# Swapping the loops over token halves and over products in the one-slot matmul helper

## Chip, cores and metric

One NeuronCore of a Trainium2 chip. The metric is the device time of one execution in microseconds; the median of three runs of the kernel before is 2221.11 us (2218.87 to 2223.14).

## The reference

A decoder trunk of two layers runs over 512 prompt tokens and 32 sample tokens (8 sequences of 4) with shared weights, all in float32, model width 1024 and feed-forward width 2816:

```
for i in range(2):
    x += 0.5 * swiglu(rms_norm(x))          # gate, up: 1024 -> 2816, down: 2816 -> 1024
    x += mixer_i(rms_norm(x))               # i = 0: conformer convolution, i = 1: gated linear attention
    x += 0.5 * swiglu(rms_norm(x))
y = rms_norm(x)                             # and the new convolution and attention states
```

The bulk of the arithmetic is the dense products of the four feed-forward blocks and of the mixers' projections.

## The kernel before

**Layout.** Activations stand feature-major in SBUF, 128 features on the partitions and all T = 544 tokens beside each other, so one matmul takes a 128x128 weight block as stationary operand and streams tokens. 544 columns do not fit one PSUM bank of 512 float32 values, so the tokens are cut into two halves of HALF = 272 columns: half c of an output block lies in bank `2 * pair + c`, and a unit of work (one output block of 128 features) owns a pair of banks. The eight banks make four pairs, and units go round them.

**Precision.** Every float32 operand is split into a high part that the matmul's fp32r type holds exactly and a low part with the rest. A product a*w is three matmuls into the same bank: w_hi*a_hi, w_hi*a_lo and w_lo*a_hi.

**Weight slots.** A slot is one block of weights of up to SLOT_K = 8 contraction steps (1024 rows x 128 columns). SyncE loads it with one DMA into `raw` (two buffers, line 386), ScalarE rounds it into `w_hi` (four buffers, line 418), VectorE writes the rest into `w_lo` (line 425) and signals `w_split`. TensorE waits for `w_split`, uses the slot and signals `w_done` on its last matmul. ScalarE waits for `w_done` before it refills a buffer, and VectorE waits for it before it evacuates the pair of banks (lines 649 and 653 in the feed-forward blocks) and signals `evac`, for which TensorE waits before a unit takes a pair again.

**Who uses a slot.** `slot_products` (line 438 is its matmul) handles units that use one slot at a time: per contraction step k six matmuls, now ordered product outside and half inside. Almost all of the kernel goes through it: the gate and up blocks after the first few (`pe_ffn`), all down blocks (three calls of 8, 8 and 6 steps on one pair), the later half of the square projections (`pe_square`) and most projections of the attention mixer. `wide_products` (line 459) handles the first units of a stage, two or four pairs at a time, and has loops of its own. Both helpers issue in program order on TensorE; there is no planner, and the orders on the other engines are written out by hand in their own blocks, tied to TensorE by the semaphores above.

**A place with another order.** In the convolution mixer, `taps` multiplies 512 token columns by diagonal weights (lines 925 and 930), 18 matmuls or more in a row into one bank, each with a weight block of its own, in the same fp32r type.

Of the kernel before, what the change touches and what calls it, by code (L numbers as in the profile page):

```python
# [42 lines left out]
def build(nc, x_prompt, x_sample, state_conv, state_gla, norm_ffn_pre, norm_mix, norm_ffn_post, norm_final,  # L43
# [26 lines left out]
    with ctx:  # L70
# [7 lines left out]
        def sb(name, shape, dt=F32):  # L78
            n = 4
            for d in shape[1:]:  # L80
                n *= d
            offset = taken[0]
            taken[0] += (n + 31) // 32 * 32
            return at(name, shape, dt, offset)
# [10 lines left out]
        w_hi = sb("w_hi", [P, RING, SLOT_K, P], F32R)  # L95
        w_lo = sb("w_lo", [P, RING, SLOT_K, P], F32R)
# [332 lines left out]
        def slot_products(pe, n, pair, a_hi, a_lo, nk=SLOT_K, k0=0, kt=SLOT_K, i=0, per=0, ready=None):  # L429

            pe.wait_ge(w_split, n + 1 + per * i)
            r = n % RING
            for k in range(nk):
                if ready is not None:
                    pe.wait_ge(ready[0], ready[1] + k + 1)
                for w, a in ((w_hi, a_hi), (w_hi, a_lo), (w_lo, a_hi)):
                    for c in range(2):
                        last = nc.tensor.matmul(  # L438
                            ps[:, 2 * pair + c, 0:HALF], w[:, r, k, :], a[:, k0 + k, c * HALF:(c + 1) * HALF],
                            start=(k0 + k == 0 and w is w_hi and a is a_hi),  # L440
                            stop=(k0 + k == kt - 1 and w is w_lo))
            last.then_inc(w_done, 1)
# [31 lines left out]
        def pe_ffn(pe, s):  # L474
            u0, s0 = s.up.u0, s.up.s0
            if s is f00:
                pe.wait_ge(evac, 2)
                pe.wait_ge(s_xo, 2)
                wide_products(pe, s0, [u0 % 4, (u0 + 1) % 4], xg_hi, xg_lo, (x_split, 0))

                pe.wait_ge(s_diag, TT + 1)
                bank = 2 * ((u0 + 3) % 4)
                for t in range(TT):
                    nc.tensor.matmul(ps[:, bank, t * P:(t + 1) * P], ones[:, :], rdiag[:, t, :], start=True, stop=True)
                nc.tensor.matmul(ps[:, bank + 1, 0:NS], ones[:, :], rdiag[:, TT, 0:NS], start=True, stop=True).then_inc(
                    s_stat, 1)
                slot_products(pe, s0 + 2, (u0 + 2) % 4, xg_hi, xg_lo)
                pe.wait_ge(s_r0, 1)
                slot_products(pe, s0 + 3, (u0 + 3) % 4, xg_hi, xg_lo)
            else:  # L490
                pe.wait_ge(evac, u0 - 2)
                wide_products(pe, s0, [u0 % 4, (u0 + 1) % 4], xg_hi, xg_lo, (x_split, M * s.q))
                pe.wait_ge(evac, u0)
                pe_stat(pe, s.e, (u0 + 3) % 4)
                slot_products(pe, s0 + 2, (u0 + 2) % 4, xg_hi, xg_lo)
                pe.wait_ge(s_nv, 3 * s.r + 1)
                slot_products(pe, s0 + 3, (u0 + 3) % 4, xg_hi, xg_lo)
# [1286 lines left out]
```

## Time and profile before

| | |
|---|---|
| median of 3 runs | 2221.11 us |
| profiled execution, its own time | 2221.3 us |
| its span (first to last instruction) | 2219.6 us |
| mean granted TensorE clock | 0.981 of full speed |
| TensorE busy | 2132.1 us, 16225 matmuls |
| TensorE weight loads busy | 2080.0 us, 16225 loads |
| VectorE, ScalarE, GpSimd busy | 1027.1, 732.8, 273.3 us |

Matmuls are pipelined: the duration in a row (some 290 ns) spans filling and draining the array and overlaps the next matmul, so what a matmul costs in a stream is the distance from one start to the next, not its duration. In the timeline, neighbouring instructions of one group are merged into a row with a count; a row "x2" is one product over its two halves.

### The profile page before, as it was taken

The page shows a single profiled execution, that of the slowest core. Times are in us where ns is not written, and L with a number is a line of the kernel's source. Part 1 is how long each engine was busy: PE and PEld are TensorE (multiplying, and loading weights), DVE is VectorE, ACT ScalarE, POOL GpSimd, SP SyncE. Part 2 cuts the span into 40 slices and gives each one's busy share as a digit, 9 for nine tenths or more (in the row PEclk, how much of TensorE's full clock was granted, in tenths as well). Part 3 has the DMA queues.
Part 4 walks back from the last instruction along what each step waited for, and adds up shares of the span by engine and source line. Part 5 has one row for each costly group of instructions (what it writes and reads, how often), then busy time and mean ns, then how long its engine had stood idle before and what let it go on. Part 6 is the DMA issues. An engine that isn't in the chain of part 4 may idle for free.

```text
span 2219.6 us, 39410 instructions
## 1 busy us (share of the span) xinstructions
PE 2132.1 (96%) x16225; PEld 2080.0 (94%) x16225; DVE 1027.1 (46%) x1266; ACT 732.8 (33%) x1132; POOL 273.3 (12%) x222
## 2 busy tenths in 40 slices
PE   8999999888789999999999999999999899999997
PEld 8999999878679999999999999999987799999997
DVE  4444433289966444433254443233455464444322
ACT  5222222376754222222232222222333242222222
POOL 0000001168823000001100000121000030000000
PEclk9999999988899999999999999999999999999999
DMA  4332233311103323322233223332224133332321
GB/s 139 91 89 85 83 88 88 97 39 57 39 24 95 95 85 88 91 82 84 82 98 92 85 85 87 88 91 77 67 58 142 58 96 95 90 90 85 95 79 67
DMA packets 338765, 185.67 MB, mean 84 GB/s; under 512 B 6012, under 2 KB 334942, under 8 KB 338668
## 3 DMA queue, kind: packets, MB, share of 16 engines
q1 hardware_dynamic: 335228, 172.78, 26.9%
q0 software_dynamic: 3200, 11.64, 1.6%
q8 instruction: 60, 0.98, 0.2%
q14 instruction: 21, 0.17, 0.0%
q10 hardware_dynamic: 256, 0.10, 0.0%
HBM read 177.29 MB, written 8.05 MB: 84 GB/s over the span
## 4 chain that ended last, share of the span: by engine, by line
PE 84%; DVE 10%; issue 3%; ACT 2%; DMA 1%; POOL 0%; ACTq 0%; SPq 0%; DVEq 0%
PE ps L438 76%; PE ps L459 4%; DVE ps L1464 3%; DVE w_lo L425 1%; DVE prod L1505 1%; ACT w_hi L418 1%; PE ps L1115 1%; DMA hist_in<-in_state_conv 0%; PE ps L1121 0%; DVE cv L1511 0%; PE ps L1054 0%; DMA pin<-in_gla_onorm_g 0%; PE ps L1062 0%; DVE x L1542 0%; DVE cv L1513 0%
## 5 line engine op out<-in xcount | busy, mean ns | idle before, releaser
L438 PE MATMUL ps<-xg_hi,w_hi 128*128 128x272 f32 x3344 | 696.9, 290 | 4.2 <-DVE tb L1479 2.2
L438 PE MATMUL ps<-xg_hi,w_lo 128*128 128x272 f32 x3344 | 693.6, 289 | 0.0
L438 PE MATMUL ps<-xg_lo,w_hi 128*128 128x272 f32 x3344 | 691.1, 288 | 0.0
L418 ACT ACTIVATE w_hi<-raw 128x1024 fp32r<-128x1024 f32 x329 | 347.7, 1059 | 1020.7 <-PE ps L438 970.3
L425 DVE TENSOR_TENSOR w_lo<-raw,w_hi 128x1024 fp32r<-128x1024 f32 x329 | 425.8, 1296 | 446.3 <-ACT w_hi L418 445.8
L438 PEld LDWEIGHTS ps<-xg_hi,w_hi 128*128 128x128 f32 x3344 | 528.6, 189 | 7.6 <-DVE tb L1479 2.6
L438 PEld LDWEIGHTS ps<-xg_lo,w_hi 128*128 128x128 f32 x3344 | 527.2, 189 | 0.0
L438 PEld LDWEIGHTS ps<-xg_hi,w_lo 128*128 128x128 f32 x3344 | 523.6, 189 | 0.0
L438 PE MATMUL ps<-h_hi,w_hi 128*128 128x272 f32 x1536 | 318.2, 288 | 1.7 <-DVE x L1542 0.9
L438 PE MATMUL ps<-h_hi,w_lo 128*128 128x272 f32 x1536 | 317.9, 288 | 0.0
L438 PE MATMUL ps<-h_lo,w_hi 128*128 128x272 f32 x1536 | 316.7, 288 | 0.0
L438 PEld LDWEIGHTS ps<-h_hi,w_hi 128*128 128x128 f32 x1536 | 241.5, 188 | 2.2 <-DVE x L1542 1.1
L438 PEld LDWEIGHTS ps<-h_lo,w_hi 128*128 128x128 f32 x1536 | 241.4, 188 | 0.0
L438 PEld LDWEIGHTS ps<-h_hi,w_lo 128*128 128x128 f32 x1536 | 239.8, 189 | 0.0
L653 DVE TENSOR_TENSOR tb<-ps,rB 128x544 f32<-128x544 f32 x88 | 63.8, 725 | 298.3 <-PE ps L438 298.3
L805 POOL TENSOR_TENSOR pool_sum<-pool_sum,tap_prod 128x512 f32<-128x512 f32 x89 | 136.0, 1528 | 56.8 <-ACT tap_prod L1260 44.5
L546 POOL TENSOR_TENSOR acc<-x 128x544 f32<-128x544 f32 x5 | 5.5, 1094 | 915.8 <-DVE x L670 854.2
L600 ACT ACTIVATE h_hi<-tb 128x544 f32 x88 | 58.0, 659 | 178.5 <-DVE tb L658 178.5
L649 DVE TENSOR_TENSOR ta<-ps,rB 128x544 f32<-128x544 f32 x88 | 63.8, 725 | 107.5 <-PE ps L438 106.6
L660 DVE TENSOR_TENSOR h_lo<-tb,h_hi 128x544 f32 x88 | 63.8, 725 | 83.9 <-ACT h_hi L600 83.9
L550 POOL TENSOR_TENSOR sqt<-x 128x544 f32<-128x544 f32 x35 | 38.3, 1095 | 315.8 <-DVE x L670 288.4
L925 PE MATMUL ps<-u_hi,diag 128*128 128x512 f32 x120 | 45.0, 548 | 29.8 <-ACT u_hi L1252 29.8
(266 smaller groups left out, 1506.0 us busy)
## 6 DMA issues: line engine op xcount, KB each, us to landing
raw<-in_ffn_w_gate SPq DMA_DIRECT2D x88, 512.0 KB, 3.8
raw<-in_ffn_w_up SPq DMA_DIRECT2D x88, 512.0 KB, 3.8
raw<-in_ffn_w_down SPq DMA_DIRECT2D x64, 512.0 KB, 4.0
raw<-in_gla_w_in SPq DMA_DIRECT2D x25, 512.0 KB, 3.8
raw<-in_ffn_w_down SPq DMA_DIRECT2D x32, 384.0 KB, 3.3
raw<-in_conv_w_pw SPq DMA_DIRECT2D x24, 512.0 KB, 4.0
raw<-in_gla_w_out SPq DMA_DIRECT2D x8, 512.0 KB, 4.0
st<-in_state_gla POOLq DMA_DIRECT2D x4, 1024.0 KB, 9.6
```

The source lines that it names most:

```text
L418: nc.scalar.activation(w_hi[:, n % RING], raw[:, n % RAW], ACT.Copy).then_inc(w_high, 1)
L425: nc.vector.tensor_tensor(w_lo[:, n % RING], raw[:, n % RAW], w_hi[:, n % RING].bitcast(F32), ALU.subtract).then_inc(w_split, 1)
L438: last = nc.tensor.matmul(ps[:, 2 * pair + c, 0:HALF], w[:, r, k, :], a[:, k0 + k, c * HALF:(c + 1) * HALF], start=(k0 + k == 0 and w is w ...
L459: last = nc.tensor.matmul(ps[:, 2 * pair + c, 0:HALF], w[:, r, k, :], a[:, k, c * HALF:(c + 1) * HALF], start=(k == 0 and w is w_hi and a ...
L550: nc.gpsimd.tensor_tensor(sqt[:, :], src[:, m, :], src[:, m, :], ALU.mult).then_inc(p_acc, 1)
L600: nc.scalar.activation(h_hi[:, 2 * i + p, :], tb[:, p, :], ACT.Copy).then_inc(h_high, 1)
L649: nc.vector.tensor_tensor(halves(ta[:, p, :]), bank_pair(pair), halves(rB[:, :]), ALU.mult).then_inc(evac, 1)
L653: nc.vector.tensor_tensor(halves(tb[:, p, :]), bank_pair((pair + 1) % 4), halves(rB[:, :]), ALU.mult).then_inc(evac, 1)
L660: nc.vector.tensor_tensor(h_lo[:, 2 * i + p, :], tb[:, p, :], h_hi[:, 2 * i + p, :].bitcast(F32), ALU.subtract).then_inc(h_split, 1)
L805: nc.gpsimd.tensor_tensor(pool_sum[:, m % 2, :], pool_sum[:, m % 2, :], tap_prod[:, k % PRODS, :], ALU.add).then_inc(c_padd, 1)
L925: last = nc.tensor.matmul(ps[:, 4 + m % 2, :], diag[:, diag_slot(m, j), part, :], u_hi[:, m % 2, j:j + SEQ], start=(j == 0 and part == 0), ...
L1464: last = nc.vector.scalar_tensor_tensor(out=ps[:, bank, :], in0=uext[:, m, j:j + SEQ], scalar=tap(j, m), in1=ps[:, bank, :], op0=ALU.mult, ...
```

## The change

In `slot_products` the loop over the two halves moves outside the loop over the three products. Per contraction step the six matmuls were (product, half) hh0 hh1 hl0 hl1 lh0 lh1, where hh is w_hi*a_hi, hl is w_hi*a_lo, lh is w_lo*a_hi; they become hh0 hl0 lh0 hh1 hl1 lh1. Each bank still receives the same products in the same order, the first matmul still carries `start`, and the last one issued is still lh1, which carries the signal. `wide_products` is left as it is.

```
             for k in range(nk):
                 if ready is not None:
                     pe.wait_ge(ready[0], ready[1] + k + 1)
-                for w, a in ((w_hi, a_hi), (w_hi, a_lo), (w_lo, a_hi)):
-                    for c in range(2):
+                for c in range(2):
+                    for w, a in ((w_hi, a_hi), (w_hi, a_lo), (w_lo, a_hi)):
                         last = nc.tensor.matmul(
                             ps[:, 2 * pair + c, 0:HALF], w[:, r, k, :], a[:, k0 + k, c * HALF:(c + 1) * HALF],
                             start=(k0 + k == 0 and w is w_hi and a is a_hi),
```

## Rows read from the trace of the kernel before

**Rows 1.** The page: span, busy time of each engine, granted clock in 40 slices.

```profile
span 2219.6 us, 39410 instructions
...
PE 2132.1 (96%) x16225; PEld 2080.0 (94%) x16225; DVE 1027.1 (46%) x1266; ACT 732.8 (33%) x1132; POOL 273.3 (12%) x222
...
PEclk9999999988899999999999999999999999999999
```

**Rows 2.** The chain that ended last, by engine and by line.

```profile
PE 84%; DVE 10%; issue 3%; ACT 2%; DMA 1%; POOL 0%; ACTq 0%; SPq 0%; DVEq 0%
...
by line: PE ps L438 76.0%; PE ps L459 3.8%; DVE ps L1464 3.1%; issue 2.5%; DVE w_lo L425 1.5%; DVE prod L1505 1.2%; ACT w_hi L418 1.0%; PE ps L1115 0.6%; DMA hist_in<-in_state_conv 0.5%; PE ps L1121 0.4%; DVE cv L1511 0.4%; PE ps L1054 0.3%
```

**Rows 3.** Instruction groups of line 438: busy us, mean ns, idle before.

```profile
L438 PE MATMUL ps<-xg_hi,w_hi 128*128 128x272 f32 x3344 | 696.9, 290 | 4.2 <-DVE tb L1479 2.2
L438 PE MATMUL ps<-xg_hi,w_lo 128*128 128x272 f32 x3344 | 693.6, 289 | 0.0
L438 PE MATMUL ps<-xg_lo,w_hi 128*128 128x272 f32 x3344 | 691.1, 288 | 0.0
...
L438 PEld LDWEIGHTS ps<-xg_hi,w_hi 128*128 128x128 f32 x3344 | 528.6, 189 | 7.6 <-DVE tb L1479 2.6
...
L438 PE MATMUL ps<-h_hi,w_hi 128*128 128x272 f32 x1536 | 318.2, 288 | 1.7 <-DVE x L1542 0.9
L438 PE MATMUL ps<-h_hi,w_lo 128*128 128x272 f32 x1536 | 317.9, 288 | 0.0
L438 PE MATMUL ps<-h_lo,w_hi 128*128 128x272 f32 x1536 | 316.7, 288 | 0.0
```

**Rows 4.** The chain in order of time, four longest pieces: start us, us, what.

```profile
33.96 384.95 PE ps L438 x3072
...
708.78 384.85 PE ps L438 x3072
...
1106.60 384.86 PE ps L438 x3072
...
1817.20 285.63 PE ps L438 x2280
```

**Rows 5.** Line 438 in a stretch of 100 us: busy, granted clock, DMA share, GB/s.

```profile
1200.00:1300.00 100.00, 100.00 (x801) 100.00 (x800) 1.00 0.30 89
```

**Rows 6.** Timeline of TensorE, eight contraction steps: start us, us, line, group.

```profile
1200.39 0.41 PE L438 MATMUL ps<-xg_hi,w_hi 128*128 128x272 f32 x2
1200.64 0.41 PE L438 MATMUL ps<-xg_lo,w_hi 128*128 128x272 f32 x2
1200.90 0.41 PE L438 MATMUL ps<-xg_hi,w_lo 128*128 128x272 f32 x2
1201.15 0.41 PE L438 MATMUL ps<-xg_hi,w_hi 128*128 128x272 f32 x2
1201.40 0.41 PE L438 MATMUL ps<-xg_lo,w_hi 128*128 128x272 f32 x2
1201.64 0.41 PE L438 MATMUL ps<-xg_hi,w_lo 128*128 128x272 f32 x2
...
1206.41 0.41 PE L438 MATMUL ps<-xg_hi,w_hi 128*128 128x272 f32 x2
```

**Rows 7.** Who waited for whom: us in total, times, longest us.

```profile
ACT w_hi L418 <- PE ps L438: 970.3, 276, 5.9
...
DVE w_lo L425 <- ACT w_hi L418: 445.8, 277, 25.3
DVE tb L653 <- PE ps L438: 298.3, 81, 3.7
```

**Rows 8.** Timeline of TensorE, first channel block of the convolution's taps.

```profile
450.86 2.95 PE L925 MATMUL ps<-u_hi,diag 128*128 128x512 f32 x12
453.64 1.55 PE L930 MATMUL ps<-u_lo,diag 128*128 128x512 f32 x6
455.04 0.42 PE L438 MATMUL ps<-xg_hi,w_hi 128*128 128x272 f32 x2
```

**Rows 9.** The same stretch: TensorE busy, granted clock, DMA share, GB/s.

```profile
450.80:455.10 4.30, 4.30 (x21) 1.00 0.00 0
```

More of the change, by code:

```diff
@@ L435, in slot_products @@
                     pe.wait_ge(ready[0], ready[1] + k + 1)
-                for w, a in ((w_hi, a_hi), (w_hi, a_lo), (w_lo, a_hi)):
-                    for c in range(2):
+                for c in range(2):
+                    for w, a in ((w_hi, a_hi), (w_hi, a_lo), (w_lo, a_hi)):
                         last = nc.tensor.matmul(
```

## The prediction

> **What bounds the kernel now.** I read the page's totals first. TensorE is busy for 2132.1 of 2219.6 us, and there are exactly as many weight loads as matmuls, 16225 of each [rows 1]. A busy row of matmuls overlaps its neighbour, so this says only that TensorE hardly ever stands idle, not how fast it streams. The chain that ended last says where the end comes from: line 438, the line of the change, is 76.0% of it [rows 2], which is 0.760 x 2219.6 = 1687 us. The changed line has 3 x 3344 + 3 x 1536 = 14640 matmuls [rows 3], or 2440 contraction steps of six.
>
> The chain in order of time gives the price of one matmul. Three pieces hold 3072 matmuls in 384.95, 384.85 and 384.86 us, a fourth 2280 in 285.63 us [rows 4]: each comes to 125.3 ns per matmul, with nothing else in the chain between them. So some 1687 / 0.1253 = 13460 of the 14640 stand on the path (2243 steps of six), and the others lie in the convolution and attention stages where other engines end the wait. The granted clock in such a stretch is 1.00, the 2.4 GHz level, with 801 matmuls in 100 us [rows 5]. At one column per cycle 272 columns would take 272 / 2.4 = 113.3 ns; the stream runs 12.0 ns above that. What these 12 ns are is the question of this change, because nothing else in the program is touched. The timeline shows that the step from one product pair to the next is 0.25 us whichever product it is [rows 6].
>
> The other engines have room. ScalarE waits 970.3 us in total for line 438 to release weight buffers, and VectorE 298.3 us for its products to evacuate [rows 7]. They follow TensorE.
>
> **The change, part by part.** Nothing is removed and nothing added: the same 14640 matmuls with the same 14640 weight loads, the same operands, the same six per step. No DMA, no instruction of SP or POOL and no wait moves. The wait for the slot stands before the six, and so does the wait for the activation block where there is one; both already cover all operands of the step, so w_lo being read third instead of fifth can't meet an unfinished split. The signal stays on lh1, which stays last, so refills and evacuations are released where they are now: cost nothing, and no cover is needed for it. Bank c = 0 gets its final product three matmuls (0.38 us) sooner, but nobody is told, so this earns nothing either. Three things differ inside the step.
>
> *One: neighbours in the same bank.* Now every matmul follows one into the other bank. Afterwards hh0-hl0, hl0-lh0, hh1-hl1 and hl1-lh1 are neighbours in one bank, four of six. No row of line 438 shows that order, so I bound it by the nearest row, the convolution's taps: same type, 128x128 weights, 18 matmuls of 512 columns in a row into one bank. They run from 450.86 to 455.04 us [rows 8], 4.18 / 18 = 232.2 ns each, at granted clock 1.00 [rows 9], against 512 / 2.4 = 213.3. That is 18.9 ns above the column time, where the bank-switching stream has 12.0. If the excess is a fixed sum per matmul, the same bank costs at most 18.9 - 12.0 = 6.9 ns. If the excess grows with the columns, the switching stream scaled to 512 would take 125.3 x 512 / 272 = 235.9 ns, the same-bank stream is 3.7 ns better, and scaled back to 272 columns that is 2.0 ns gained. On the path 13460 x 4/6 = 8970 neighbours are concerned: the ends are +62 us and -18 us. I take 0, because the two readings have opposite signs and the true law of the excess (two points, one of 272 and one of 512 columns) most plausibly lies between them: a straight line with an intercept leaves nothing for the bank.
>
> *Two: weight changes.* Now the stationary block differs from the one before twice per step (hl1 to lh0, and lh1 to the next hh0). Afterwards it differs four times, since lh0 stands between two w_hi products. The timeline has both kinds today. A step from the hh row to the hl row holds two starts without a change, the other two kinds of step hold one change each. Over the eight steps from 1200.39 to 1206.41 us [rows 6] the eight hh-to-hl distances sum to 2.02 us, the sixteen others to 4.00 us: 252.5 ns without a change, 250.0 with one. A change costs -2.5 ns, with some 3 ns of uncertainty from rows rounded to 0.01 us, so at most about +0.5. Two more per step on 2243 steps of the path: ends +2 and -12 us (taken at -2.5). I take 0, since the taps of [rows 8] change weights at every matmul and stream no better for it. The reason is plain in the groups: a load is issued for every matmul, changed or not [rows 1, 3].
>
> The Trainium skill has a rule against this change: TensorE: Matmul & The Clock Gate, section Step-by-step, says that loading apart from computing lets one load weights once and matmul repeatedly. By it the old order would need two loads per step and the new one four. The trace doesn't bear it out for this program, which issues six loads in a step; by the rule the sum would be positive, by the row it is 0.
>
> *Three: what streams while what loads.* Now the stream of a_hi runs beside the coming w_hi three times in six, and each other pairing once. Afterwards a_hi beside w_hi four times, a_lo beside w_lo twice. No pairing is new in kind, and all of them lie within the 0.24 to 0.26 us per pair of [rows 6]: 0, inside the bounds of the second point.
>
> The sum is 0 + 0 + 0. The profiled execution took 2221.3 us with a span of 2219.6, 0.2 us from the median of 2221.11 us. I predict 2221.2 us.
>
> **The rivals.** About 0.2%, 4.4 us, is what a measurement of this kernel can tell from no change; divided over 8970 neighbours that is 0.5 ns per matmul. So this is a sharp question, and small effects count.
>
> *Slower by the bank:* a matmul that accumulates into the bank just written pays a fixed fee. For it: the taps' excess of 18.9 against 12.0 ns. Against it: 512 columns are more columns, and their activations are read at shifted offsets, which the dense stream doesn't do. At the full 6.9 ns it is 2221.2 + 62 = 2283 us; it decides from 0.5 ns upwards. Chance 0.06.
>
> *Slower by the weights:* a changed block costs more than a repeated one, but today each change is followed by at least one repeat that absorbs it; with lh0 alone between two changes, it no longer is. For it: a load's row lasts 189 ns [rows 3], longer than the distance of 125.3, so loads must overlap. Against it: the taps change at every matmul, and their excess is at most 6.9 ns more with 512 columns to hide a load in. At 3 ns for each of 2 x 2243 more changes it is 13 us, 2235 us; it decides from 1 ns upwards. Chance 0.06. This is also where the skill's rule of loading once would show.
>
> *Faster by the bank:* the 12.0 ns are the price of going to the other bank after each matmul. Four of six would no longer pay it: 8970 x 12.0 = 108 us, 2114 us. For it: every matmul of line 438 switches, so nothing in that line contradicts it. Against it: the taps never switch in a run of 18 and are further above their column time, not nearer. Chance 0.07, smaller gains such as the 18 us above (2203 us) included.
>
> A change that doesn't do what it says is hard to picture here, as the program is issued in the written order; it would give the forecast's time.
>
> **How the numbers follow.** Forecast, no measurable change: 0.78. The two slower rivals 0.12, the faster one 0.07, and 0.03 for causes that I don't name, two thirds of it slower, where there is more room for mishap. That makes faster 0.08, same 0.78, slower 0.14. The forecast's own band is 2216.8 to 2225.6 us. It holds slightly under 8 in 10, so the range reaches a little into the others: down by 7 us, a gain of 0.8 ns per neighbour in a bank, to 2214; up by 12 us, a fee of 1.3 ns per neighbour or most of the 3 ns per change, to 2233.
>
> **What would show it.** Right: the long pieces of the chain still hold 3072 matmuls in 384.9 us; the line's groups keep their counts; the timeline of a step shows single hh, hl, lh rows twice with starts 0.125 us apart; ScalarE's wait for line 438 stays near 970 us. Bank fee: the distances hh to hl and hl to lh grow while lh0 to hh1 stays at 125. Weight fee: the distances at lh, before and behind, grow while hh to hl stays. Bank gain: hh to hl and hl to lh fall towards 113 ns, and ScalarE's wait shrinks. The prediction is wrong if the pieces of 3072 differ from 384.9 us by more than about 1.0 us (4.4 x 3072 / 13460).

## The result, and the profile after

The changed kernel takes 2232.54 us (2230.46 to 2237.08, five runs) against 2220.93 us (2217.31 to 2223.14) of the kernel before: a ratio of 1.0055, interval 1.0042 to 1.0068. It is slower by 11.6 us, small, but well outside what a measurement can mistake.

The page of the changed kernel, its span and busy times, answers to [rows 1]:

```profile
span 2230.7 us, 39410 instructions
...
PE 2139.9 (96%) x16225; PEld 2087.8 (94%) x16225; DVE 1030.2 (46%) x1266; ACT 732.3 (33%) x1132; POOL 269.8 (12%) x222
```

The counts are the old ones, down to the last instruction: nothing was added, and nothing else was set off. Its chain in order of time, against [rows 4], shows where the time went:

```profile
32.96 387.50 PE ps L438 x3072
...
711.63 387.41 PE ps L438 x3072
...
1112.01 387.43 PE ps L438 x3072
...
1825.81 287.53 PE ps L438 x2280
```

Each piece of 3072 matmuls has 2.55 to 2.57 us more than its partner, the piece of 2280 has 1.90 us more. All four give 0.83 to 0.84 ns per matmul, 126.1 for 125.3, or 5.0 ns per contraction step of six. Over the 13460 matmuls of the path that is 13460 x 0.83 = 11.2 us; the profiled spans differ by 2230.7 - 2219.6 = 11.1 us. The four pieces together, 11496 matmuls, already hold 9.6 us of it. So there is no new wait and no stage to look for: the stream itself is slower, by the same amount in all four pieces that `slot_products` feeds.

The granted clock of such a stretch is still 1.00, the 2.4 GHz level, with 796 matmuls in 100 us for the 801 of [rows 5]:

```profile
1200.00:1300.00 100.00, 100.00 (x796) 100.00 (x794) 1.00 0.31 89
```

The waits of the other engines only stretch with the stream (970.3 us in [rows 7]):

```profile
ACT w_hi L418 <- PE ps L438: 981.4, 276, 5.9
```

And the timeline of a contraction step, against [rows 6], shows the new order as single rows, hh hl lh and again hh hl lh:

```profile
1203.02 0.29 PE L438 MATMUL ps<-xg_hi,w_hi 128*128 128x272 f32 x1
1203.14 0.29 PE L438 MATMUL ps<-xg_lo,w_hi 128*128 128x272 f32 x1
1203.27 0.29 PE L438 MATMUL ps<-xg_hi,w_lo 128*128 128x272 f32 x1
1203.40 0.29 PE L438 MATMUL ps<-xg_hi,w_hi 128*128 128x272 f32 x1
1203.52 0.29 PE L438 MATMUL ps<-xg_lo,w_hi 128*128 128x272 f32 x1
1203.65 0.29 PE L438 MATMUL ps<-xg_hi,w_lo 128*128 128x272 f32 x1
```

A fee of under a nanosecond per matmul can't be read off single starts that are printed to 10 ns. The pieces of 3072 show it: within either of these two runs they agree to 0.1 us. They are the measure in all that follows, old order 384.9 us, new order 387.4 us. Where no interval stands beside a whole time, or only pieces are shown, the kernel was run once.

### The profile page after: what moved, and what is told of

Same layout as the page of the kernel before. It is cut to its first block, busy times and chain, and to the rows that moved or that the text cites. A ratio compares the mean times of both kernels' runs of the same rounds, so it can differ in the third digit from the quotient of the medians.

```text
span 2230.7 us, 39410 instructions
## 1 busy us (share of the span) xinstructions
PE 2139.9 (96%) x16225; PEld 2087.8 (94%) x16225; DVE 1030.2 (46%) x1266; ACT 732.3 (33%) x1132; POOL 269.8 (12%) x222
## 4 chain that ended last, share of the span: by engine, by line
PE 84%; DVE 10%; ACT 2%; issue 2%; DMA 1%; POOL 0%; SPq 0%; ACTq 0%; DVEq 0%
PE ps L438 77%; PE ps L459 4%; DVE ps L1464 3%; DVE w_lo L425 2%; DVE prod L1505 2%; ACT w_hi L418 1%; PE ps L1115 1%; PE ps L1121 0%; DMA hist_in<-in_state_conv 0%; DVE cv L1511 0%; PE ps L1054 0%; DMA pin<-in_gla_onorm_g 0%; PE ps L1062 0%; DVE x L1542 0%; DVE u_lo L1498 0%
## 5 line engine op out<-in xcount | busy, mean ns | idle before, releaser
L438 PE MATMUL ps<-xg_hi,w_hi 128*128 128x272 f32 x3344 | 971.3, 290 | 5.1 <-DVE tb L1479 2.2
L438 PE MATMUL ps<-xg_lo,w_hi 128*128 128x272 f32 x3344 | 967.8, 289 | 0.0
L438 PE MATMUL ps<-xg_hi,w_lo 128*128 128x272 f32 x3344 | 967.5, 289 | 0.0
L438 PEld LDWEIGHTS ps<-xg_hi,w_hi 128*128 128x128 f32 x3344 | 631.5, 189 | 7.9 <-issue 3.2
L438 PEld LDWEIGHTS ps<-xg_lo,w_hi 128*128 128x128 f32 x3344 | 630.6, 189 | 0.8
L438 PEld LDWEIGHTS ps<-xg_hi,w_lo 128*128 128x128 f32 x3344 | 630.8, 189 | 0.0
L438 PE MATMUL ps<-h_hi,w_hi 128*128 128x272 f32 x1536 | 444.4, 289 | 1.7 <-DVE x L1542 0.9
L438 PE MATMUL ps<-h_lo,w_hi 128*128 128x272 f32 x1536 | 443.9, 289 | 0.0
L438 PE MATMUL ps<-h_hi,w_lo 128*128 128x272 f32 x1536 | 443.7, 289 | 0.0
L438 PEld LDWEIGHTS ps<-h_hi,w_lo 128*128 128x128 f32 x1536 | 289.0, 188 | 0.0
## 6 DMA issues: line engine op xcount, KB each, us to landing
raw<-in_ffn_w_down SPq DMA_DIRECT2D x32, 384.0 KB, 3.4
```

What stands on the lines that cost most here:

```text
L438: last = nc.tensor.matmul(ps[:, 2 * pair + c, 0:HALF], w[:, r, k, :], a[:, k0 + k, c * HALF:(c + 1) * HALF], start=(k0 + k == 0 and w is w ...
```

## The experiments

### Bank, weights or streams

Three theories stood at the start. The new order has four neighbours per step in the same bank where the old one has none; it has four changes of the stationary block where the old one has two; and a second half never follows the first half of the same tile any more. Four kernels take these apart. The first, second and fourth edits below are made in the new kernel, the third in the old one; `...` marks lines of an edit that are not shown.

**Banks alternate, the rest as in the new order.**

```
-                for c in range(2):
-                    for w, a in ((w_hi, a_hi), (w_hi, a_lo), (w_lo, a_hi)):
+                hh, hl, lh = (w_hi, a_hi), (w_hi, a_lo), (w_lo, a_hi)
+                order = ((hh, 0), (hl, 1), (lh, 0), (hh, 1), (hl, 0), (lh, 1))
+                for n_mm, ((w, a), c) in enumerate(order):
...
```

> The six matmuls of a step in the order hh0 hl1 lh0 hh1 hl0 lh1: the weight blocks follow each other as in the changed kernel (four changes of block per step), and so does what streams while what loads, but every matmul goes to the other bank than the one before, as in the old kernel. Bank theory (1.25 ns for each same-bank neighbour, none left here): long pieces of the chain 384.9 us for 3072 matmuls, about 2221 us. Weight theory (2.5 ns for each of the two added changes): 387.4 us, about 2232 us. Stream theory (1.7 ns for each lost pair hh0-hh1, hl0-hl1, lh0-lh1 in which the second half follows the first of the same tile): 387.4 us, about 2232 us.

Measured: 2221.41 us, ratio 0.9997 (0.9988 to 1.0007). The chain of this run, in which the matmul stands at line 441:

```profile
710.30 384.85 PE ps L441 x3072
...
1108.12 384.86 PE ps L441 x3072
```

This is the old time exactly, with four weight changes per step and no half that follows its first half. The weight theory and the stream theory as I had put it are gone. Had I stopped here, the bank would have looked guilty.

**Same-bank neighbours with two weight changes.**

```
...
+                order = ((hh, 0), (hl, 0), (hh, 1), (hl, 1), (lh, 1), (lh, 0))
...
```

> Order hh0 hl0 hh1 hl1 lh1 lh0: four same-bank neighbours of six, counting lh0 to the next step's hh0, as in the changed kernel, but only two changes of weight block per step, as in the old one. Bank theory: 387.4 us per 3072 matmuls, about 2232 us. Weight theory: 384.9 us, about 2221 us. Stream theory (no second half follows its first half): 387.4 us, about 2232 us.

Measured: 2223.93 us, ratio 1.0016 (1.0007 to 1.0026). Its chain:

```profile
709.43 385.69 PE ps L441 x3072
...
1108.08 385.71 PE ps L441 x3072
```

It fits none of the three theories: 0.85 us per piece above the old order, a third of the new order's fee, with as many same-bank neighbours.

**One bank for everything, old order of operands.**

```
-                            ps[:, 2 * pair + c, 0:HALF], w[:, r, k, :], a[:, k0 + k, c * HALF:(c + 1) * HALF],
+                            ps[:, 2 * pair, 0:HALF], w[:, r, k, :], a[:, k0 + k, c * HALF:(c + 1) * HALF],
...
```

> The old order of operands throughout, but both halves are summed into the first bank of the pair, so all six matmuls of a step are same-bank neighbours; the second bank keeps old contents (half of the outputs are not the reference's). Bank theory: 6 x 1.25 = 7.5 ns per step, 512 steps in a piece of 3072, so 384.9 + 3.8 = 388.7 us, about 2238 us. Weight theory and stream theory: 384.9 us, about 2221 us.

Measured: 2221.57 us, ratio 1.0000 (0.9990 to 1.0009). Its chain:

```profile
709.72 384.85 PE ps L438 x3072
...
1107.54 384.86 PE ps L438 x3072
```

All six matmuls of a step go to one bank, and not a hundredth of a microsecond is to be seen. The bank theory is gone, and with it two of the prediction's rivals.

**The new order's weights on the old order's streams.**

```
...
+                order = ((w_hi, a_hi, 0), (w_hi, a_hi, 1), (w_lo, a_lo, 0), (w_hi, a_lo, 1), (w_hi, a_hi, 0),
+                         (w_lo, a_hi, 1))
...
```

> The old order of streams and banks (a_hi0 a_hi1 a_lo0 a_lo1 a_hi0 a_hi1, banks alternating), but the stationary blocks follow each other as in the changed kernel, w_hi w_hi w_lo w_hi w_hi w_lo, so that some products are replaced by others and the sums differ. Weight theory: 387.4 us per 3072 matmuls, about 2232 us. Bank theory and stream theory: 384.9 us, about 2221 us.

Measured: 2221.31 us, ratio 1.0000 (0.9990 to 1.0009). Its chain, with the matmul at line 439:

```profile
707.71 384.85 PE ps L439 x3072
...
1105.53 384.86 PE ps L439 x3072
```

The order of the weight blocks has no price, by a second run.

What do the three runs at the old time share, that the other two don't? The halves of the streams go 0 1 0 1 0 1 in all three. The halves differ in tokens, but also in where they begin in SBUF, and from here on addresses are the theory. The numbers that follow are worked out from the shapes in the kernel. A half is 272 x 4 = 1088 bytes = 17 x 64, a block of 544 columns 34 x 64, a weight block of 128 columns 8 x 64. The bases of the high and low tiles lie whole multiples of 256 bytes apart (17408 for the normed activations, 47872 for the hidden ones, 16384 for the weights), so high and low are alike modulo 256 and all weight blocks begin at one phase. Call the start address, counted in 64-byte pieces modulo four, the phase of a stream; relative to the weight blocks, half c of step k begins at phase 2k + c. The old order runs through 0 1 0 1 0 1, then 2 3 2 3 2 3; the new one through 0 0 0 1 1 1, then 2 2 2 3 3 3.

### Other start addresses, same halves

The slice of the second half is moved; the first stays.

```
-                            ps[:, 2 * pair + c, 0:HALF], w[:, r, k, :], a[:, k0 + k, c * HALF:(c + 1) * HALF],
+                            ps[:, 2 * pair + c, 0:HALF], w[:, r, k, :], a[:, k0 + k, c * 256:c * 256 + HALF],
```

This edit is made in the old kernel and in the new one. Two more kernels have the old order with 240 or 224 in place of 256. The second half then streams other tokens as well.

> The old order, but the second half streams columns 256 to 527 in place of 272 to 543 (272 columns as before, of other tokens, so half of each product belongs to shifted tokens). In bytes a half is 1088 = 17 x 64 and a block of 544 columns 2176; the second half now starts 1024 bytes after the first, not 1088. Address theory: what counts is where a stream starts against the one before it, in 64-byte pieces; five of six streams now start at the phase of the one before, as four of six do in the changed kernel, and each repeat costs 4.98 / 4 = 1.25 ns: 512 x 5 x 1.25 = 3.2 us more per piece of 3072, 388.1 us. Half theory (a stream of the same tokens as the one before costs, whatever its address): 384.9 us.

> The new order, the second half streams columns 256 to 527 (other tokens, same count). Address theory: both halves have the same phase, so the order of the halves can't matter, and this takes what the old order with columns from 256 takes, to within 0.1 us per piece of 3072 (388.1 us by the simple price). Half theory: the fee of the new order stays whole, 387.4 us against 384.9 us of the old order with the same columns.

> The old order, the second half streams columns 240 to 511 (other tokens, same count); it starts 960 bytes after the first, 15 x 64. Address theory with a fee for a repeated phase alone: no repeats, 384.9 us; if a step forward and a step back in phase have different prices, it moves off 384.9 us here. Half theory: 384.9 us.

> The old order, the second half streams columns 224 to 495 (other tokens, same count); it starts 896 bytes after the first, 14 x 64, an even number of 64-byte pieces. Address theory by 128 bytes (two phases): as with 256 columns, every stream but none forward starts at the phase of the one before, 388.1 us or more. Address theory by 256 bytes (four phases): one repeat in six, 385.5 us, if only repeats cost. Half theory: 384.9 us.

The chain of the old order with columns from 256:

```profile
33.99 385.80 PE ps L438 x3072
...
712.18 387.40 PE ps L438 x3072
...
1112.55 387.42 PE ps L438 x3072
```

and of the new order with columns from 256:

```profile
32.82 385.80 PE ps L438 x3072
...
710.40 387.40 PE ps L438 x3072
...
1110.77 387.42 PE ps L438 x3072
```

The two agree piece by piece to 0.01 us, even in the odd first piece. Once both halves begin at the same phase, the order of the halves costs nothing, as the address theory has it; the half theory wanted 2.55 us between them. The level I had expected, 388.1 us, was wrong, so a price per repeated phase is not the law. The chain with columns from 240:

```profile
706.71 380.60 PE ps L438 x3072
...
1100.28 380.60 PE ps L438 x3072
```

It is 4.26 us per piece under the old order, and the whole run took 2205.03 us for 2223.68 of the kernel before beside it. Nothing but the start address of every second stream was changed, by 128 bytes, and with it which tokens it reads. The fee for repeated phases alone, with its 384.9 us, is missed here again. From 224 it is the new order's time again, which none of the expected values (384.9, 385.5, 388.1 us or more) was:

```profile
710.91 387.40 PE ps L438 x3072
...
1111.28 387.42 PE ps L438 x3072
```

So start addresses count, in both directions, and more than two phases do, as 240 and 272 are alike modulo 128 bytes. That it is the addresses and not the tokens is shown further on, where addresses move and tokens stay.

### Against each other, or against the weights

Next the halves were swapped in the old and in the new kernel, with nothing left out, and the weight tiles were moved.

```
-                    for c in range(2):
+                    for c in (1, 0):
```

> The old order, but within each product the second half goes first: hh1 hh0 hl1 hl0 lh1 lh0. Nothing is left out. Address theory with prices by step of phase (four phases of 64 bytes, a half begins 17 x 64 bytes behind the first, a step of k 34 x 64): from the old order (4 steps forward, 2 back, 751.7 ns per contraction step) and the run with columns from 240 (2 forward, 4 back, 743.3 ns) a step forward costs 126.7 ns and a step back 122.5. Here four go back (1 to 0 three times, and 0 to the next step's 1, which is 3 phases on) and wait, two forward: 743.3 ns, 380.6 us per piece of 3072, about 2202 us in all. Half theory, or a gain in the 240 run that came from its shorter reach of columns: 384.9 us, about 2221 us.

Measured: 2246.75 us, ratio 1.0109 (1.0092 to 1.0126), the slowest of all. Its chain:

```profile
716.13 390.82 PE ps L438 x3072
...
1119.92 390.79 PE ps L438 x3072
```

A plain miss: I expected 380.6. A price per step of phase, from stream to stream, is not the law.

> The new order with the second half first: hh1 hl1 lh1 hh0 hl0 lh0. Nothing is left out. Address theory by prices of steps (repeat of phase 125.8 ns from the new order, back 122.5): four repeats and two back, 4 x 125.8 + 2 x 122.5 = 748.3 ns per contraction step, 383.1 us per piece of 3072, about 2213 us, faster than the old order. Half theory, in which repeating a half costs: 387.4 us, about 2232 us, as the new order.

Measured: 2228.51 us, ratio 1.0027 (1.0017 to 1.0038). Its chain, 387.49 in the first piece and then:

```profile
710.17 385.70 PE ps L438 x3072
...
1108.82 385.71 PE ps L438 x3072
```

The 383.1 of the step prices is missed here too.

Then the weight tiles, and all tiles allocated behind them, begin 64 or 128 bytes further on:

```
+        taken[0] += 64
         w_hi = sb("w_hi", [P, RING, SLOT_K, P], F32R)
```

> The old order, but both weight tiles (and the tiles allocated behind them) begin 64 bytes further on in SBUF. If only the streams' addresses against each other matter: 384.9 us per piece of 3072. If the fee comes from a stream meeting the load of the next weights, so that the weights' address counts as well: it moves, by up to the 4 us that lie between the orders measured so far (380.6 to 387.5).

> The same with 128 bytes. Streams alone: 384.9 us. Streams against loads with a period of 256 bytes: it moves; with a period of 128 bytes: 384.9 us here, while 64 bytes moved it.

The chain of the old order with the weights 64 bytes on:

```profile
33.88 382.39 PE ps L439 x3072
...
706.48 384.00 PE ps L439 x3072
...
1103.44 384.01 PE ps L439 x3072
```

and 128 bytes on:

```profile
710.75 384.86 PE ps L439 x3072
...
1108.57 384.87 PE ps L439 x3072
```

The streams of the first of these are untouched, and yet it moves. So the weights' address counts, and a stream is to be seen against the weight blocks (the tiles behind them, which moved too, are ruled out by the next run). With 128 bytes nothing moves. My text expected a move from a period of 256 bytes and would take this for a period of 128; that was an oversight. A step of k moves the streams by 128 bytes modulo 256, so this shift only lets even and odd steps change places, and the run can't tell the two periods apart. The runs with columns from 240 and 272 do.

That makes a sharp test. Swapping the halves gives the phases 1 0 1 0 1 0, 3 2 3 2 3 2. Weights moved on by one piece are streams moved back by one: 0 3 0 3 0 3, 2 1 2 1 2 1. These are the phases of the run with columns from 240. Two edits, one that alone costs 5.9 us per piece and one that alone gains 0.8 to 2.6, would together have to gain 4.26.

> The old order with the second half first, and both weight tiles 64 bytes further on. Nothing is left out. Relative-address theory: the price hangs on where a stream lies against the load of the weights beside it, modulo 256 bytes. Moving the weights by 64 bytes on is moving all streams by 64 bytes back; the streams of this kernel then lie against the weights exactly as in the run with columns from 240 (a step forward of 128 bytes in k only swaps even and odd steps). So it must cost what that run cost, 743.3 ns per contraction step, 380.6 us per piece of 3072, about 2202 us, although each of the two edits alone gave 390.8 and 383.5. Theory of the streams alone: 390.8 us as without the shift, about 2247 us. Two separate effects that add: 390.8 - 1.4 = 389.4 us, about 2240 us.

Measured: 2202.76 us (2201.63 to 2205.07) against 2222.06, ratio 0.9917 (0.9904 to 0.9931). Its chain:

```profile
704.57 380.59 PE ps L439 x3072
...
1098.12 380.61 PE ps L439 x3072
```

The 380.6 is hit to 0.01 us. It also settles two rivals that were still open: this kernel streams its own tokens, and the run with columns from 240 had every tile in its old place. And since nothing is left out of this kernel, it is also a better one than either: 0.83% faster than the kernel before.

> The new order with both weight tiles 64 bytes further on; nothing is left out. If the order's fee is one of streams against loads, it is another one here: the distance to the old order with the same shift (382.4 to 384.0 us per piece of 3072) is not the 2.55 us it was without the shift, and may have another sign. If the order has a price of its own, whatever the addresses, 382.4 + 2.55 to 384.0 + 2.55, so 385 to 386.6 us.

The chain of the new order with the same shift:

```profile
709.93 387.42 PE ps L439 x3072
...
1110.31 387.41 PE ps L439 x3072
```

387.4, as without the shift. The distance to the old order with the same shift is 3.4 us and more, not 2.55, so the order has no price of its own. My text didn't foresee the equality, but the phases do: 3 3 3 0 0 0, 1 1 1 2 2 2 is the new order's own round of twelve, begun three matmuls earlier.

The last two runs, one of each order, thin the loads out. The edit halves the weight columns of each load, and with them what each matmul writes.

```
-                            ps[:, 2 * pair + c, 0:HALF], w[:, r, k, :], a[:, k0 + k, c * HALF:(c + 1) * HALF],
+                            ps[0:64, 2 * pair + c, 0:HALF], w[:, r, k, 0:64], a[:, k0 + k, c * HALF:(c + 1) * HALF],
```

> The old order, but each matmul of the changed helper loads only 64 of the 128 weight columns and writes 64 of the 128 output partitions (half of each output block is left out). The streams are as before. If the 12 ns above the 113.3 ns of the columns come from loads that stand in the streams' way: half of them or more goes, 119 ns or less per matmul, 366 us or less per piece of 3072. If they belong to the streams or to the issue of a matmul: 125.3 ns, 384.9 us.

> The new order with the same half loads (half of each output block is left out). Streams against loads: the fee of the new order, 0.83 ns per matmul, shrinks or goes with the loads, within 0.4 ns of the old order with half loads (1.3 us per piece of 3072). A price of the order of the streams alone: it stays 0.83 ns, 2.55 us per piece.

The chain of the old order with half loads:

```profile
708.44 382.29 PE ps L438 x3072
...
1103.69 382.30 PE ps L438 x3072
```

and of the new order:

```profile
704.95 382.30 PE ps L438 x3072
...
1100.22 382.31 PE ps L438 x3072
```

With half the weight columns, the fee of the new order is gone to 0.01 us, as expected if loads and streams meet. But of the 12.0 ns above the column time only 0.8 went (382.3 / 3072 = 124.4 ns), where I had set 119 ns or less against no change at all: most of it stays with half the columns. A half load is also shorter, 134 to 137 ns in its groups for the 189 of [rows 3]:

```profile
L438 PEld LDWEIGHTS ps<-xg_hi,w_hi 128*64 128x64 f32 x3344 | 436.6, 137 | 9.2 <-issue 2.7
```

Load, load time and output are halved together, so these runs don't say which of them takes the fee away; and the two orders agree here in their totals alone, as the next part shows. They are a weaker sign for the loads than the shift of the weights.

### Read together

Phases of the streams against the weights, over an even and an odd contraction step, and the pieces of 3072:

| kernels | phases | us |
|---|---|---|
| old order; banks alternate; one bank; weights only; old, weights +128 | 0 1 0 1 0 1, 2 3 2 3 2 3 (or even and odd swapped) | 384.9 |
| new order; new, weights +64 | 0 0 0 1 1 1, 2 2 2 3 3 3 (or begun three earlier) | 387.4 |
| old from 240; second half first with weights +64 | 0 3 0 3 0 3, 2 1 2 1 2 1 | 380.6 |
| old from 256; new from 256 | 0 0 0 0 0 0, 2 2 2 2 2 2 | 385.8, then 387.4 |
| same bank, two changes | 0 0 1 1 1 0, 2 2 3 3 3 2 | 385.7 |
| old from 224 | 0 2 0 2 0 2, 2 0 2 0 2 0 | 387.4 |
| second half first | 1 0 1 0 1 0, 3 2 3 2 3 2 | 390.8 |
| second half first, new order | 1 1 1 0 0 0, 3 3 3 2 2 2 | 387.5, then 385.7 |
| old, weights +64 | 3 0 3 0 3 0, 1 2 1 2 1 2 | 382.4, then 384.0 |

Kernels in one row agree piece by piece to 0.03 us, although they differ in bank, weight order, tokens or loop order. They agree in more than the total. The traces keep every start to 1 ns, where the timeline prints 10 ns, so the distance from one matmul to the next can be averaged by its place in the round, over a whole piece. In the new order these distances run from 120.0 to 130.0 ns, with a fixed value at each place. Kernels in one row have the same distance at every place to 0.1 ns: all five of the first row, set off by whole steps where needed; columns from 240 and the second half first with weights +64; old and new order from 256, on both levels; and the new order with and without the shift, set off by three places. (In the last pair this holds for three of the four pieces; in the second piece the shifted kernel keeps the distances that the unshifted one has in its first and fourth, with the same sum.) An equal total alone says less: the new order and the old one from 224 share 387.4 us, and the two kernels with half loads 382.3 us, but however they are laid against each other, some place differs by at least 2.4 ns in the first pair and 6.6 ns in the second.

**What is shown:** start addresses of streams and weights set the time, and sorted by phase modulo 256 bytes every equality falls into place, one of them foretold. **What stays open:** a law that gives the price of a row from its phases (the one I tried failed twice); why three rows have two levels within one run; whether the period is 256 bytes or more, as kernels in one row are alike modulo 512 bytes too, and most repeat their distances after 12 matmuls, but the old order only after 24; shifts by less than 64 bytes, which were not run; and the mechanism inside the memory or the array, into which no run here looks.

## Why the prediction was wrong

**The bound** held. Line 438 sets the end, the other engines follow, the counts stay, no wait is added: every word of that is in the profile after. The loss per matmul times the number on the path gives the whole difference.

**Point one, the bank,** at 0 was right, by the run with one bank. But its ends, +62 and -18 us, came from comparing 512 columns with 272 and laying the difference to the bank; with 272 columns the bank makes none.

**Point two, the weight changes,** at 0 was right, by two runs with four changes per step at the old time. The rule of loading once that I set against the change from the Trainium skill (TensorE: Matmul & The Clock Gate, section Step-by-step) pointed to the right sign, but not by its reason: the two extra changes cost nothing in a program that loads for every matmul anyway. The -2.5 ns per change came from the rounding of the rows: from starts to 1 ns over a whole piece the distance of a pair with one change is 0.2 ns above that of a pair without, and the lower end, 2 x 2243 x 2.5, is -11 us and not -12.

**Point three is the step that failed:** "No pairing is new in kind". I counted by tile names, and by names it is so. The pairing that counts is of addresses. In the old order the phases alternate, in the new one they come in threes, and no row of line 438 in the old trace shows a run of three. The zero had no row behind it: rows between 0.24 and 0.26 us per pair leave 20 ns open where 1.7 ns per pair came, and its bounds were borrowed from the second point. Its size was 11.2 us, where 0.5 ns per neighbour was known to be enough to decide. The old trace could have warned: by starts to 1 ns, the way from lh1 to the next hh0, always the same tiles, banks and change of block, takes 129.2, 125.8, 124.2 and 126.7 ns in four steps that follow each other, round after round. Tile names can't explain that.

**The rivals.** Both slower ones named the right side with a wrong cause; 11.2 us is 1.25 ns per same-bank neighbour or 2.5 ns per added change, which lies between "decides" and what either was given. The faster one is refuted by the run with one bank. The chance of 0.78 for no change was far too sure: I had written that half a nanosecond decides and that small effects count, and had bounds of tens of microseconds on both sides, yet put all of the weight on the point between them. The range, 2214 to 2233, holds the time by 0.5 us, and that is luck: its upper end was set for a bank fee or a weight fee, and neither exists here.

**The test I named** was the right one: pieces of 3072 off 384.9 us by more than 1.0 us. They were off by 2.55. The signs by single distances were of no use: by place they run from 120.8 to 129.2 ns in the old order already, and from 120.0 to 130.0 in the new one, so no single distance carries the fee.

The Trainium skill, TensorE: Matmul & The Clock Gate, section Step-by-step, says that loading the next tile's weights doesn't steal SBUF read bandwidth from the running matmul. The runs here differ in the small: with the same streams, moving the weight tiles by 64 bytes changes the stream by 0.3 to 0.8 ns per matmul, so the stream isn't indifferent to where the weights lie. The measurement decides; whether that is read bandwidth no run shows.

## What to carry to other kernels

When a stream of matmuls is the path and nothing else changes, an order of operands is not free just because counts, banks and waits stay: look at where each stream and each weight block begins, modulo 256 bytes, and price a reordering by running it. Average the starts by their place in the loop: that tells two causes with one total apart. Where halves begin at an odd multiple of 64 bytes, try the orders of the halves together with a shift of the weight tile by 64 bytes; here that spans 380.6 to 390.8 us for one and the same work, 2.7%, and the best pair of the two edits beat both kernels while one of them alone was the worst. A single variation of a suspected cause can acquit or convict the wrong one, as the run with alternating banks would have done.

## What was not expected of the hardware

The stream's time is quantised: 384.86, 385.71, 387.42, 380.60, 390.80 and 382.30 us lie 1, 3, -5, 7 and -3 steps of 0.85 us from the first. One step is 0.85 us / 512 = 1.67 ns per contraction step, four periods of the 2.4 GHz clock, the level granted in these stretches. By the starts to 1 ns the grain is coarser still. A round of twelve takes 1486.7 to 1526.7 ns and is always a multiple of 6.67 ns, 16 periods; the old order repeats only after 24 matmuls, in 451 times 6.67 ns, and so lies half way between two levels. The same line, fed the same way, can also stand on two levels in one run: 385.80 us in the first feed-forward block and 387.40 in the next, in two kernels alike. And sending all six matmuls of a step to one bank rather than two in turn changed a piece of 3072 by no more than 0.01 us.
